# Late division of the attention output, and retention weights staged as f32, in a hybrid decoder layer on 8 cores

## The reference, cut to what matters

```
xn = rmsnorm(x); split xn @ w_in into attention q,k,v | retention q,k,v | retention gate | merge gates A, B
A: for (window, dilation) in (128,1), (512,4), (2048,16):  p = exp(s - m) over strided causal keys
   attention = sum of the three numerators / sum of the three denominators      # per head and position
B: retention, 4 heads, chunks of 128: inner (q k^T * decay) v, plus q @ state; state = gamma*state + k^T v
   per-head RMS norm, times silu(gate)
mixer = (sigmoid(gateA) * (attention @ w_att) + sigmoid(gateB) * (retention @ w_ret)) @ w_out
```

## Time and profile before

| | us |
|---|---|
| median of three runs | 1603.39 (1602.49 to 1746.77) |
| the profiled execution's own time | 1601.79 |
| its span on the slowest core (core 1) | 1597.6 |
| spans of the other cores | 1574.9 to 1594.3 |
| PE busy | 1370.9 (86%) |
| DVE / ACT / POOL busy | 763.3 / 695.2 / 762.8 |

### The profile page before, as it was taken

How to read it: one execution, slowest core, us unless ns; L and a number is a source line. 1 busy time by engine, 2 the same in 40 slices (tenths; PEclk the granted TensorE clock), 3 DMA queues, 4 the chain that set the end, 5 groups by cost and what they waited for, 6 DMA issues and landing times.

```text
span 1597.6 us, 29878 instructions; the slowest of 8 cores (1574.9 to 1597.6 us)
## 1 busy us (share of the span) xinstructions
PE 1370.9 (86%) x10037; PEld 789.1 (49%) x10037; DVE 763.3 (48%) x1239; ACT 695.2 (44%) x1191; POOL 762.8 (48%) x874
## 2 busy tenths in 40 slices
PE   4899998888879999999999899999999736565675
PEld 2344547776744444444444444444445435454563
DVE  3787774766656556555656411111354652211122
ACT  3576668887853444434443411111233542222232
POOL 1379981333236657666756312221225645543453
PEclk9999999998999999999999999999999957887888
DMA  9747866786765769999994399875964785999985
GB/s 221 215 92 131 165 155 177 163 188 139 179 138 89 118 101 131 125 131 146 122 137 123 61 289 166 131 125 129 244 220 154 228 286 153 275 254 251 281 162 91
DMA packets 105502, 267.03 MB, mean 167 GB/s; under 512 B 43352, under 2 KB 65368, under 8 KB 98818
## 3 DMA queue, kind: packets, MB, share of 16 engines
q0 software_dynamic: 29280, 124.30, 49.7%
q1 hardware_dynamic: 76066, 140.76, 28.4%
HBM read 285.71 MB, written 116.65 MB: 252 GB/s over the span
## 4 chain that ended last, share of the span: by engine, by line
PE 69%; DMA 13%; DVE 5%; issue 4%; ACT 4%; POOL 2%; SPq 1%; another core or an unknown queue 0%; DVEq 0%; POOLq 0%; ACTq 0%
PE ps L169 69%; DMA arena<-xn,idx 8%; DMA zret<-arena 5%; DVE arena L169 4%; ACT arena L169 3%; POOL arena L169 2%; DMA cfs_sb<-cfs 1%; DVE arena L167 1%; SPq L169 1%; DMA vp<-arena 0%; DVEq L156 0%; DVE logit L169 0%; ACT L169 0%; POOLq L176 0%
## 5 line engine op out<-in xcount | busy, mean ns | idle before, releaser
L169 PE MATMUL ps<-arena 128*128 128x512 bf16 (+5 forms) x8208 | 1275.5, 313 | 78.5 <-ACT arena L169 32.5
L169 PEld LDWEIGHTS ps<-arena 128*128 128x128 bf16 (+1 forms) x8208 | 679.0, 102 | 587.1 <-issue 122.4
L169 ACT ACTIVATE arena<-ps 128x512 bf16<-128x512 f32 (+5 forms) x600 | 422.5, 719 | 450.6 <-PE ps L169 412.2
L169 POOL TENSOR_TENSOR arena<-arena 128x512 bf16<-128x512 f32 (+4 forms) x274 | 347.7, 1278 | 297.9 <-DVE arena L169 244.7
L169 DVE TENSOR_TENSOR arena<-ps,arena 128x512 f32<-128x512 f32 (+4 forms) x420 | 235.3, 572 | 347.0 <-ACT arena L169 159.8
L169 PE MATMUL ps<-cbs_sb,arena 128*128 128x128 bf16 x1408 | 131.1, 232 | 107.3 <-DMA arena<-xn,idx 69.7
L169 DVE SCALAR_TENSOR_TENSOR arena<-arena,ps 128x512 f32<-128x512 f32 x176 | 115.5, 683 | 192.3 <-PE ps L169 190.7
L169 PEld LDWEIGHTS ps<-cbs_sb,arena 128*128 128x128 bf16 x1408 | 100.7, 104 | 176.2 <-issue 147.8
L169 ACT ACTIVATE arena<-arena 128x8 f32<-128x8 f32 (+5 forms) x225 | 148.6, 665 | 59.0 <-DVE arena L169 29.1
L169 DVE TENSOR_TENSOR arena<-arena 128x1024 bf16<-128x1024 bf16 (+9 forms) x176 | 130.7, 750 | 75.7 <-ACT arena L169 68.7
L169 POOL DMA_INDIRECT out<-arena,idx x48 | 76.3, 1590 | 126.5 <-ACT arena L169 66.6
(11 more groups left out here) (60 smaller groups left out, 339.9 us busy)
## 6 DMA issues: line engine op xcount, KB each, us to landing
wb<-wexp POOLq DMA_DIRECT2D x60, 768.0 KB, 13.8
arena<-wb SPq DMA_DIRECT2D x30, 1536.0 KB, 15.4
arena<-x SPq DMA_DIRECT2D x32, 512.0 KB, 7.8
arena<-vx POOLq DMA_DIRECT2D x12, 768.0 KB, 5.1
arena<-wri POOLq DMA_DIRECT2D x8, 1024.0 KB, 23.1
zret<-arena SPq DMA_DIRECT2D x16, 512.0 KB, 19.8
arena<-zret SPq DMA_DIRECT2D x4, 2048.0 KB, 17.2
out<-arena SPq DMA_DIRECT2D x16, 512.0 KB, 9.8
```

Source lines behind the costliest of these rows:

```text
L169: ins = getattr(engobj, meth)(*a, **kw)
```

## The change

Four things are changed.

1. *Division.* Attention no longer divides. After each head SP stores the f32 numerators (`num`, 64 x 2048) and one row of denominators (`den`). In retention step 1 DVE takes the reciprocals of all denominators, gathered as 128 x 256, and they go back to DRAM (`rden`). In steps 48 to 58 of retention (column blocks 0 and 1) and during the merge (blocks 2 and 3) SP loads blocks of 128 x 512 numerators with the reciprocals broadcast over 64 rows, and DVE multiplies them into `za[c]`, eight products per block.
2. *Mask.* Only items 3 and 5 of a head have the bias matmuls; items 2 and 4 have the DVE mask.
3. *Retention weights.* SP loads them as f32 in chunks of 128 x 1024 into staging buffers, two during attention, four during retention. POOL casts them in attention (items 1 and 6 of a head, two chunks behind the load), ACT in retention (twice per step, four chunks behind). The first head's weights start one pair earlier.
4. *DMA shapes and places.* `convert` moves its half in six pieces per row instead of two, `load_wm` in pieces of 512 elements instead of 2048 and 1536. Buffers of the merge move within SBUF, `zr[0]` is loaded two steps later, and one load of 8 chunks of `za` per block gives way to the products.

```diff
-    zatt_d = nc.dram_tensor("zatt", [D, S], BF16, kind=skind).ap()
+    num_d = nc.dram_tensor("num", [D, S], F32, kind="Internal").ap()
+    den_d = nc.dram_tensor("den", [16, S], F32, kind="Internal").ap()
+    rden_d = nc.dram_tensor("rden", [16, S], F32, kind="Internal").ap()
...
-                p.dma(wb_d[e][:, cs].rearrange("p (a b) -> p a b", a=2), wexp_d[e][:, cs].rearrange("p (a b) -> p a b", a=2),
+                p.dma(wb_d[e][:, cs].rearrange("p (a b) -> p a b", a=6), wexp_d[e][:, cs].rearrange("p (a b) -> p a b", a=6),
...
+        def stage_add(dst, src, Rs):
+            for j, r_ in enumerate(Rs):
+                tasks.append((dst[:, j * 1024:(j + 1) * 1024], src[:, j * 1024:(j + 1) * 1024], r_))
+                late_res.add(id(r_))
+
+        def stage_load():
+            n = done[0]
+            if n < len(tasks) and n - done[1] < len(stg):
+                done[0] += 1
+                i = n % len(stg)
+                p.dma(stg[i], tasks[n][1], writes=[Rstg[i]], semkey=("stg", i))
+
+        def stage_cast(eng, lag):
+            n = done[1]
+            if n < done[0] and (done[0] - n >= lag or done[0] == len(tasks)):
+                done[1] += 1
...
+                if eng == "act":
+                    OP("act", "activation", out=dst, in_=stg[i], func=AF.Copy, reads=[Rstg[i]], writes=[r_])
+                else:
+                    OP(eng, "tensor_copy", out=dst, in_=stg[i], reads=[Rstg[i]], writes=[r_])
...
-        def den_shift(pr, e, hf):
...
-        def den_act(pr, hf, func, scale):
...
-        def z_out(pr, hf):
...
+        def head_out(pr, e):
+            h, r0, d0, i = 2 * pr + e, e * 64, 64 - e * 64, (2 * pr + e) % NXO
+            p.dma(num_d[h * 64:(h + 1) * 64, :], xo[i][r0:r0 + 64, :], reads=Rxo[i], writes=[Rnum[h]], semkey=("zatt", i))
+            p.dma(den_d[h:h + 1, :], xo[i][d0:d0 + 1, :], reads=Rxo[i], writes=[Rdend[h]], semkey=("xin", i))
...
-            queue.append((pr, eh, n_, S_item(pr, eh, kind, j, n_ in (2, 3, 4, 5))))
+            queue.append((pr, eh, n_, S_item(pr, eh, kind, j, n_ in (3, 5))))
...
+            if n_ in (1, 6):
+                stage_cast("pool", 2)
+                stage_load()
...
+        def div_load(c):
+            pr, i = dv[0] % 8, dv[0] % len(nb)
+            dv[0] += 1
+            cs = slice(c * 512, c * 512 + 512)
+            p.dma(nb[i], num_d[pr * 128:(pr + 1) * 128, cs], reads=Rnum[2 * pr:2 * pr + 2], writes=[Rnb[i]], semkey=("vp", i))
+            for e in range(2):
+                p.dma(rb[i][e * 64:(e + 1) * 64, :], rden_d[2 * pr + e, cs].partition_broadcast(64), reads=[Rrden], writes=[Rrb[i][e]],
...
+        def div_mul(c):
...
+            OP("dve", "tensor_tensor", out=za[c][:, pr, :], in0=nb[i], in1=rb[i], op=ALU.mult, reads=[Rnb[i]] + Rrb[i],
...
-            load_cast(d[:, 0:2048], wm_d[fc][:, 0:2048], 1, Rwm[i][0], ("wm", i, 0))
-            load_cast(d[:, 2048:5120], wm_d[fc][:, 2048:5120], 2, Rwm[i][1], ("wm", i, 1))
+            load_cast(d[:, 0:2048], wm_d[fc][:, 0:2048], 4, Rwm[i][0], ("wm", i, 0))
+            load_cast(d[:, 2048:5120], wm_d[fc][:, 2048:5120], 6, Rwm[i][1], ("wm", i, 1))
...
-                if 1 <= s_ % 16 <= 4 and 2 <= s_ // 16 + 1 < 4:
-                    load_head_weight(s_ // 16 + 1, s_ % 16 - 1)
+                if s_ % 16 == 1 and 2 <= s_ // 16 + 1 < 4:
+                    load_head_weights(s_ // 16 + 1)
                 stage_A(s_)
+                stage_cast("act", 4)
+                stage_load()
...
+                stage_cast("act", 4)
+                stage_load()
+                if s_ == 1:
+                    den_rec()
+                if s_ == 45:
...
+                    for u_ in range(4):
+                        div_load(0)
+                if 48 <= s_ < 59:
+                    for _ in range(1 + (s_ % 2 == 0 and s_ < 57)):
+                        div_mul(dv[1] // 8)
+                        if dv[0] < 16:
+                            div_load(dv[0] // 8)
...
-        areset(56 * KB)
-        for c in (1, 2):
-            z_alloc(c)
-            load_za(c)
-            load_zr(c)
+        zr_alloc(1, 64)
+        load_zr(1)
+        div_bufs((56, 60, 124))
+        for u_ in range(3):
+            div_load(2)
+        za_alloc(2, 80)
+        zr_alloc(2, 88)
+        load_zr(2)
...
                 piece(fc, c, n, 4 * (un % 2), 0, "pool")
+                pi = 5 * un + n
+                if pi >= 4 and dv[1] < 16 and (pi % 2 == 0 if dv[1] < 8 else pi % 3 == 0):
+                    div_mul(2 + dv[1] // 8)
+                    if dv[0] < 16:
+                        div_load(2 + dv[0] // 8)
```

More of the change, by code:

```diff
@@ L341, in MM @@
         def MM(out, lhsT, rhs, start, stop, reads, writes, **kw):
+            assert not late_res or all(id(r_) not in late_res for r_ in reads)
             return p.op("pe", "matmul", (out,), dict(lhsT=lhsT, rhs=rhs, start=start, stop=stop, **kw), reads, writes)
@@ L763, in build_nc @@
         xo = [alloc([128, S], F32, Rxo[i]) for i in range(NXO)]
-        zb = [x_.bitcast(BF16)[:, 0:S] for x_ in xo]
-        Rden = [[p.res(f"den{i}_{e}") for e in range(2)] for i in range(2)]
-        den = [alloc([128, S // 2], F32, Rden[i]) for i in range(2)]
-        Rzatt = [p.res(f"zatt{i}") for i in range(16)]
+        Rnum = [p.res(f"num{h}") for h in range(16)]
+        Rdend = [p.res(f"dend{h}") for h in range(16)]
         slot = [0]
@@ L895, in load_head_weight @@
             w = (wq_r, wk_r, wv_r, wg_r)[j][i]
[L896 removed]
+            stage_add(w.rearrange("p k n -> p (k n)"), wri_d[h, :, c0:c1], Rwr[i][j])
         def load_head_weights(h):
[L899 removed]
+            for j in (0, 1, 3, 2):
                 load_head_weight(h, j)
         def wr_alloc1(i, j):
[L903 removed]
+            (wq_r, wk_r, wv_r, wg_r)[j].append(alloc([128, 8, 256 if j < 2 else 512], BF16, Rwr[i][j]))
         def wr_alloc(i):
@@ L929, in pv_next @@
             if n_ == NB - 1:
-                todo.setdefault(g + 1, []).append(lambda: (osb_copy(pr, eh, 3), den_shift(pr, eh, 1)))
-                if eh == 1:
-                    for hf in range(2):
-                        for lag, f in ((1, lambda hf=hf: den_act(pr, hf, AF.Ln, 1.0)), (3, lambda hf=hf: den_act(pr, hf, AF.Exp, -1.0)),
-                                       (5, lambda hf=hf: z_out(pr, hf) if pr < 7 else deferred.append(lambda: z_out(pr, hf)))):
-                            todo.setdefault(g + lag + 4 * hf, []).append(f)
+                todo.setdefault(g + 1, []).append(lambda: (osb_copy(pr, eh, 3), head_out(pr, eh)))
         for pr in range(2):
@@ L975, in build_nc @@
             g += 1
-        deferred = []
         for g in sorted(todo):
@@ L993, in build_nc @@
         wr_alloc(1)
+        stb = []
+        for i in range(4):
+            areset((176 + 4 * i) * KB)
+            stb.append(alloc([128, 1024], F32, [Rstg[i]]))
+        stage_init(stb)
         areset(112 * KB)
@@ L1021, in build_nc, with den_rec, div_bufs @@
         assert apos[0] <= 167 * KB, apos[0]
+        areset(92 * KB, 96 * KB)
+        Rdall = p.res("dall")
+        dall = alloc([128, 256], F32, [Rdall])
+        Rrden = p.res("rden")
+        p.dma(dall, den_d.rearrange("h (a b) -> (h a) b", a=8), reads=Rdend, writes=[Rdall], semkey="rawtab")
+        Rnb = [p.res(f"nb{i}") for i in range(4)]
+        Rrb = [[p.res(f"rb{i}_{e}") for e in range(2)] for i in range(4)]
+        nb, rb, dv = [], [], [0, 0]
+        def den_rec():
+            OP("dve", "reciprocal", out=dall, in_=dall, reads=[Rdall], writes=[Rdall])
+            p.dma(rden_d.rearrange("h (a b) -> (h a) b", a=8), dall, reads=[Rdall], writes=[Rrden], semkey="gqkb")
+        def div_bufs(at):
+            assert dv[0] == dv[1]
+            del nb[:], rb[:]
+            for i, k in enumerate(at):
+                areset(k * KB)
+                nb.append(alloc([128, 512], F32, [Rnb[i]]))
+                rb.append(alloc([128, 512], F32, Rrb[i]))
+            dv[:] = [0, 0]
+        def div_load(c):
[5 more added lines that the diff above has]
+                p.dma(rb[i][e * 64:(e + 1) * 64, :], rden_d[2 * pr + e, cs].partition_broadcast(64), reads=[Rrden], writes=[Rrb[i][e]],
+                      semkey=(("zero", i // 2, i % 2), ("qz", i // 2, i % 2, False))[e])
+        def div_mul(c):
+            pr, i = dv[1] % 8, dv[1] % len(nb)
+            dv[1] += 1
+            OP("dve", "tensor_tensor", out=za[c][:, pr, :], in0=nb[i], in1=rb[i], op=ALU.mult, reads=[Rnb[i]] + Rrb[i],
+               writes=[Rza[c][pr]])
         INNER = ps[:, 3, 0:128]
@@ L1143, in build_nc @@
         za, zr = {}, {}
-        Rza = [[p.res(f"za{c}")] for c in range(NG)]
+        Rza = [[p.res(f"za{c}_{k}") for k in range(8)] for c in range(NG)]
         Rzr = [[p.res(f"zr{c}")] for c in range(NG)]
@@ L1210, in build_nc @@
         RmT = [[p.res(f"mT{c}_{k}") for k in range(8)] for c in range(NG)]
-        mT = [alloc([128, 8, 512], BF16, RmT[c]) for c in range(NG)]
```

(4 more changed lines are left out.)

74 lines of the change are left out of this document (37 added, 37 removed).

## The result

The changed kernel takes 1688.1 us (median) against 1606.2 for the kernel before, a ratio of 1.051 (95% interval 1.044 to 1.057). It is slower; the forecast was 1575, in a range of 1554 to 1597.

What follows compares the result with a forecast made beforehand. TensorE was taken to bound retention and merge, so gain was sought in attention. From the profiled 1601.8 us, -25 - 10 - 1 + 3 + 5 = -28 gave 1573.8, or 1575 as the runs' median; range 1554 to 1597.

Steps and rivals of the forecast that it cites:

- Denominators, -25: Attention: dropping the denominators' Ln/Exp, products and GpSimd copies saves 25 us, bounds 25 and 31.
- 6.5 us of unexplained TensorE waits: Attention's 14 slower heads: TensorE waits without a cause in the profile, taken to stay, which lowers 31.4 us to 24.9.
- Mask, -10: Attention: two biased items per head lose their bias matmuls, saving 10 us, bounds 4 and 12.
- the first step: Attention: without denominators the 14 heads fall from 13.50 us towards a clean head of 11.26; 25 us taken.
- Retention weights, +3: Retention: weights staged through SP and cast on ScalarE cost 3 us, bounds -4 and +25.
- 53 of 54 us, it just fits: Retention: DMA work for conversions (31 us), chunks (19) and stores (3) in the eight steps of a head's chunks.
- Rival 4: Retention: staged loads lose turns to conversion packets, a chunk takes 6.8 us; some 100 us lost, about 1665; chance 0.07.
- Division, late retention, 0: Late retention: half of the 32 VectorE products run there, VectorE 59% busy; only the merge's start called tight.
- Division, start of the merge, +5: Merge start: loads of 11.8 MB at 272 GB/s end at 953 us, needed at 948; +5, bounds 0 and +15.
- rival 3: Merge: its start starves, costing +15 us instead of +5, total 1584; chance 0.10.
- Finer pieces, 0: Conversions and merge weights: 512-element pieces cost nothing, as each packet holds the same bytes; bounds a quarter of conversion time.
- Stores and loads of attention, 0: Attention: f32 numerator stores add 13 us of DMA, 168 in about 180; nothing taken, bounds 0 to 10 us.

Runs made afterwards that it cites:

- den_only: Changed kernel with retention weights loaded as before, late division left out and four biased items per head restored; ratio 0.987 to the kernel before, attention 208.8 us.
- rb_rows: Changed kernel with reciprocal loads reading 64 different numerator rows in place of one row 64 times; merge 345.9 us against 367.0.
- loads_nowait: Changed kernel with all division loads kept, but the VectorE products take other operands and so don't wait for them; merge 350.5 us against 367.0.
- before_split: Kernel before with only the finer pieces of expert conversions and merge weights; ratio 0.999.
- compact3: Kernel before with the mask change, a compact bf16 division in attention, and attention's six conversions moved to the merge's second half; ratio 1.007.
- compact5: Kernel before with the mask change, a compact bf16 division in attention, and attention's six conversions moved to retention's last steps; ratio 0.985, 1574.1 us.
- bias_only: Kernel before with the mask part alone: items 2 and 4 of a head get VectorE mask products in place of bias matmuls; ratio 1.003.

## Why the prediction was wrong, step by step

- *Denominators, -25.* Right in mechanism and near in size: -20 (`den_only`). The 6.5 us of unexplained TensorE waits that the sum kept became 12.1; what they are stays open.
- *Mask, -10.* The clean head did fall to 10.7, and the gain shows only behind the first step, on whose clean head it was reckoned. It measured 4.5 us by the stage and 8 by the ratios; it may be mis-sized, but no run here excludes 10.
- *Retention weights, +3.* This step failed: +44 where the upper bound was 25. The sum "53 of 54 us, it just fits" was a sum of work, and a short one: a conversion writes 768 KB, so the 6.84 MB of the earlier trace rows are 8.7 conversions of 5.9 us each, six of them are 35 us and not 31, and the sum is 57 of 54. Above all it said nothing on when a chunk lands. Beside conversions it took 16.8 us where its cast was due after 13.5, and still 16 to 20 us at half the rate; without them, 4.6. Rival 4 named this and priced it at 100; it came to less than half, 19 us of ScalarE waits per head where it had 41. Its price supposed a software packet before every row of a chunk, 0.648 of each 0.848 us or 76% of the engines; from 600 to 650 us the software queue had 53.4%. That its total, 1665, is the nearest to the measured one is luck: the rest of the loss is the division's. The chance of 0.07 was too small also because I priced one such wait; the change added two more in VectorE's order.
- *Division, late retention, 0.* Failed: +21. I wrote that only the merge's start is tight, having checked VectorE's busy share and not its order. A product whose reciprocals are 14.6 us late holds up every evacuation behind it (TensorE waited 12.4 us for VectorE at one time).
- *Division, start of the merge, +5.* Failed, and so did rival 3, which capped it at 15: +43. I took the rate of the earlier trace rows, 272 GB/s, for loads that no row of before contained. Reads of one row are slow (`rb_rows`, -21), and the products in VectorE's order pass a part of each late load on to TensorE: 102 us of VectorE's waits became 39 of TensorE's. Taking this wait out brings only 17 back (`loads_nowait`), because GpSimd then waits for the kept weights' copy-out.
- *Finer pieces, 0.* Right (`before_split`). The figure of the Trainium skill weighed beside it ("DMA: Bandwidth & Descriptors", SWDGE vs HWDGE vs iDMA: a packet of preferably 4096 B) does not show: the packets stayed at 5.5 KB (3.93 MB in 720). The 0.43 us reckoned from it was also too low: 0.648 us x 4096 B / 5.5 KB is 0.48.
- *Stores and loads of attention, 0.* Not tested alone; the -20 above holds them. `compact3` to `compact5` show that attention with a compact division is sensitive to DMA: 11 us for six conversions.

## What to carry to other kernels

A transfer fits when it lands before the instruction that waits for it, not when the bytes fit the stretch: look up the landing times beside the same traffic, and what stands behind the waiting instruction in its engine's order. Before putting a wait into the queue of an engine that evacuates PSUM, assume that TensorE will pay for a part of it. And background transfers belong in stretches whose DMA share the profile shows low: moved to one at 0.40, six conversions gave attention's 11 us; in two busier places the merge and the projection paid more than that for them.

## What the runs showed of the hardware

- Reading one 2 KB DRAM row into 64 partitions costs more than reading 64 rows: for 64 such loads (4,096 rows) 40 us of all 16 engines in the median over the cores, an estimated 0.15 us more per row, in the stretch above. No row ahead of the prediction shows such a load.
- TensorE's granted clock falls in long waits and stays low for a little behind them. Around the wait of 26.9 us that ended at 1013.49 us (stretches as in the earlier trace rows):

```profile
984.00:1012.00 28.00, 2.60 (x13) 0.97 (x10) 4.56 (x7) 1.27 (x2) 1.81 (x1) 0.61 0.88 197
1012.00:1020.00 8.00, 6.51 (x21) 2.54 (x22) 2.31 (x4) 1.27 (x2) 1.78 (x2) 0.65 1.00 132
1020.00:1052.00 32.00, 31.92 (x148) 14.27 (x146) 4.92 (x8) 2.64 (x4) 5.17 (x7) 1.00 0.99 126
```

So parts of the first two were at 1.2 GHz in place of 2.4. Most of that falls into the wait itself, where nothing runs; of the 8 us around its end some 2 us were lost (an estimate: 0.35 of the 6.5 us worked there). A wait costs a little more than its length.
- The mask products that VectorE took over cost as much as the matmuls they replaced (`bias_only`, 1.003) while ScalarE still turned the denominators over, and gained 4.5 to 8 us once it did not.
